# Layer 1 of a two-layer encoder: all four condition vectors weighed by VectorE, slabs and ring turns in another order

## What is computed

```
for layer in range(2):
    mod = silu(c) @ w_ada[layer] + b_ada[layer]          # 1024 -> 6 x 1024
    sh1, sc1, g1, sh2, sc2, g2 = split(mod, 6)
    h = rmsnorm(x, mix_norm_g[layer]) * (1 + sc1) + sh1
    y = even_mixer(h) if layer == 0 else odd_mixer(h)     # attention + convolution | differential attention
    x = x + g1 * y
    h = rmsnorm(x, ffn_norm_g[layer]) * (1 + sc2) + sh2
    x = x + g2 * hierarchical_moe(h)                      # 32 experts, 2 for each token
```

## Time and profile before

| what | us |
|---|---|
| median of three runs | 1234.25 |
| the profiled execution's own time | 1233.65 |
| its span, first to last instruction | 1231.6 |
| TensorE busy | 891.0 (72%) |
| VectorE busy | 340.9 (28%) |
| ScalarE busy | 170.4 (14%) |
| weights' DMA queue, share of 16 engines | 95.2% |

### The profile page before, as it was taken

How to read it: one execution, slowest core, us unless ns; L and a number is a source line. 1 busy time by engine, 2 the same in 40 slices (tenths; PEclk the granted TensorE clock), 3 DMA queues, 4 the chain that set the end, 5 groups by cost and what they waited for, 6 DMA issues and landing times.

```text
span 1231.6 us, 14489 instructions
## 1 busy us (share of the span) xinstructions
PE 891.0 (72%) x5990; PEld 431.9 (35%) x5990; DVE 340.9 (28%) x879; ACT 170.4 (14%) x409; POOL 23.8 (2%) x70
## 2 busy tenths in 40 slices
PE   6999998657474756566799999967465565665647
PEld 5867453122221312121278555533121212121212
DVE  3298445121211111111133653521111111202111
ACT  1123340000000000000033253400000000000000
POOL 1001100000000000000000100000000000000000
PEclk9999999787887868787899999989787878888778
DMA  9999989999999999999996838999999999999997
GB/s 349 397 404 408 412 350 423 427 429 427 427 429 427 428 428 429 427 429 428 405 408 233 321 137 317 378 426 427 428 427 427 428 429 428 428 430 426 428 423 283
DMA packets 62136, 490.05 MB, mean 398 GB/s; under 512 B 5600, under 2 KB 6001, under 8 KB 39552
## 3 DMA queue, kind: packets, MB, share of 16 engines
q1 hardware_dynamic: 59568, 486.56, 95.2%
q10 hardware_dynamic: 2512, 2.69, 0.6%
HBM read 488.18 MB, written 1.05 MB: 397 GB/s over the span
## 4 chain that ended last, share of the span: by engine, by line
DMA 49%; PE 42%; DVE 3%; SPq 2%; ACT 2%; issue 1%; POOL 0%; DVEq 0%; ACTq 0%
PE psum L1598 42%; DMA weight_ring<-in_moe_w_up 16%; DMA weight_ring<-in_moe_w_down 16%; DMA weight_ring<-in_moe_w_gate 16%; SPq L489 2%; DMA weight_ring<-in_w_ada 1%; ACT phase_region L893 1%; DVE h_or_mix_T L1111 0%; PE psum L1697 0%; POOL phase_region L660 0%; DVE ada_partials L1522 0%; DVE phase_region L1554 0%; ACT phase_region L1012 0%; DVE phase_region L1081 0%; DVE h_or_mix_T L1243 0%
## 5 line engine op out<-in xcount | busy, mean ns | idle before, releaser
L1598 PE MATMUL psum<-weight_ring,h_or_mix_T 128*32 128x512 f32 (+1 forms) x2240 | 383.3, 709 | 231.7 <-DMA weight_ring<-in_moe_w_gate 142.0
L1598 PEld LDWEIGHTS psum<-weight_ring,h_or_mix_T 128*32 128x32 f32 (+1 forms) x2240 | 118.7, 136 | 478.5 <-issue 476.6
L1598 PE MATMUL psum<-weight_ring,ada_partials 128*32 128x512 f32 x1024 | 138.9, 699 | 77.9 <-DMA weight_ring<-in_moe_w_down 72.9
L1598 PE MATMUL psum<-phase_region 128*128 128x128 f32 (+5 forms) x816 | 154.3, 351 | 6.1 <-DVE phase_region L1424 1.6
L1598 PEld LDWEIGHTS psum<-phase_region 128*128 128x128 f32 (+2 forms) x816 | 97.9, 188 | 79.5 <-issue 53.8
L1598 PE MATMUL psum<-h_or_mix_T,weight_ring 128*128 128x256 f32 (+1 forms) x528 | 115.0, 374 | 2.8 <-DVE h_or_mix_T L1111 2.7
L1598 PEld LDWEIGHTS psum<-h_or_mix_T,weight_ring 128*128 128x128 f32 x528 | 97.3, 190 | 17.5 <-DVE h_or_mix_T L1111 1.9
L1598 PEld LDWEIGHTS psum<-weight_ring,ada_partials 128*32 128x32 f32 x1024 | 38.8, 126 | 165.4 <-issue 158.2
L1424 DVE TENSOR_TENSOR phase_region<-psum,gate_rows 128x512 f32<-128x512 f32 x32 | 22.1, 692 | 224.7 <-PE psum L1598 224.7
L1411 DVE SCALAR_TENSOR_TENSOR phase_region<-phase_region,psum 128x512 f32<-128x512 f32 x16 | 11.0, 687 | 236.9 <-ACT phase_region L925 236.9
L1416 DVE SCALAR_TENSOR_TENSOR ada_partials<-phase_region,psum 128x512 f32<-128x512 f32 x16 | 16.8, 1050 | 209.3 <-PE psum L1598 209.3
(11 more groups left out here) (220 smaller groups left out, 479.5 us busy)
## 6 DMA issues: line engine op xcount, KB each, us to landing
weight_ring<-in_moe_w_up SPq DMA_DIRECT2D x64, 2048.0 KB, 20.5
weight_ring<-in_moe_w_gate SPq DMA_DIRECT2D x62, 2048.0 KB, 19.9
weight_ring<-in_moe_w_down SPq DMA_DIRECT2D x62, 2048.0 KB, 20.0
weight_ring<-in_w_ada SPq DMA_DIRECT2D x10, 3072.0 KB, 20.3
weight_ring<-in_odd_w_in SPq DMA_DIRECT2D x6, 2048.0 KB, 23.9
weight_ring<-in_w_ada SPq DMA_DIRECT2D x10, 1024.0 KB, 22.4
weight_ring<-in_w_ada SPq DMA_DIRECT2D x4, 2048.0 KB, 17.9
weight_ring<-in_even_w_in SPq DMA_DIRECT2D x3, 2048.0 KB, 21.0
```

The costliest lines, as they stand in the source:

```text
L1598: return pe.matmul(out_, lhsT, rhs, start=first, stop=last, **kw)
```

## The change

Vectors 10 and 11 go the way of 8 and 9: VectorE weighs the slab, TensorE only adds partitions. All four are now weighed between the projections, in the order 8, 9, 10, 11; their slabs, the ring's places and layer 1's turns are reordered; `gate_join` of layer 1 gives way to `keep_warm(1, 16)`. Two pieces of layer 0's mixer change place. The end of each layer loads and multiplies the last down quad in other pieces (two loads of two experts with rows 0 and 1, then left halves of rows 2 and 3, then the right side in columns 512 to 767 and 768 to 1023), and the copy into `CREP1` is gone.

```diff
-        mid_slabs = [("odd_in", 0, 1, proj_done, 26), ("odd_in", 1, 2, proj_done, 34), ("odd_in", 2, 0, proj_done, 38),
-                     ada(8, 3), ada(9, 1), ("odd_out", 0, 3, wout_done, 8), ada(10, 2), ada(11, 0)]
-        TURNS = [(1, 2, 0, 3), (1, 2, 0, 3)]
+        mid_slabs = [("odd_in", 0, 1, proj_done, 26), ada(8, 2), ("odd_in", 1, 0, proj_done, 34),
+                     ("odd_in", 2, 3, proj_done, 38), ada(9, 2), ada(10, 1), ada(11, 2), ("odd_out", 0, 1, wout_done, 8)]
+        TURNS = [(1, 2, 0, 3), (0, 2, 3, 1)]
...
-                for k in range(2):
+                for k in range(2 + L):
...
+            weigh(8, 0, 5)
+            behind_unit = {0: (8, 5, 6), 1: (8, 6, 7), 2: (8, 7, 8), 7: (9, 0, 2), 8: (9, 2, 4), 9: (9, 4, 6), 10: (9, 6, 8),
+                           11: (10, 0, 1), 12: (10, 1, 2), 13: (10, 2, 4), 14: (10, 4, 6), 15: (10, 6, 8)}
             for u in range(16):
...
-                if 8 <= u < 12:
-                    weigh(8, 2 * (u - 8), 2 * (u - 7))
-                if u == 13:
-                    take_modulation(8)
-                if u > 13:
-                    weigh(9, 2 * (u - 14), 2 * (u - 13))
-
-            weigh(9, 4, KD)
+                if u in (6, 12):
+                    take_modulation({6: 8, 12: 9}[u])
+                if u in behind_unit:
+                    weigh(*behind_unit[u])
+
+            weigh(11, 0, 5)
...
             biased(0)
+            weigh(11, 5, KD)
             biased(1)
-            take_modulation(9)
+            take_modulation(10)
...
-                if u == 14:
+                if u == 5:
                     add_rows(8)
+                if u == 12:
+                    pe.wait_ge(ada_ready, 9)
+                    add_rows(9)
...
+            pe.wait_ge(qk_rstd, 16)
+            add_rows(10)
             scores(0)
             project_values(1, AFT)
             scores(1)
-            pe.wait_ge(qk_rstd, 16)
-            add_rows(9)
...
-                if h == 3:
-                    pe.wait_ge(v_out, 4)
-                    modulation_sums(10)
...
-                if L:
-                    modulation_sums(6 * L + 5, 0, KD // 2)
-                modulation_sums(6 * L + 5, KD // 2, KD)
                 if L == 0:
+                    modulation_sums(5, KD // 2, KD)
                     keep_warm(1, 5)
+                else:
+                    pe.wait_ge(router_ready, 2 * L + 2)
+                    add_rows(11)
+                    keep_warm(1, 8)
...
-                gate_join(6 * L + 5)
+                if L == 0:
+                    gate_join(5)
+                else:
+                    keep_warm(1, 16)
...
             modulation_sums(3)
+            modulation_sums(7, 0, 3)
...
             tails(1)
-            modulation_sums(7)
+            modulation_sums(7, 3, KD)
...
+            pe.wait_ge(logs_min, NPAIR)
+            mix_out(0, 2, (0, 1))
             values(3)
-            for u in (2, 3):
-                mix_out(0, u, (0, 1))
+            mix_out(0, 3, (0, 1))
             pe.wait_ge(ada_ready, 5)
             mix_out(0, 1, (0, 1))
             pe.wait_ge(conv_added, 2)
             channel_sum(S).then_inc(conv_var, 1)
```

The new end of a layer on TensorE (`rows` multiplies one row of four experts, `combine_cols` is `combine` for a slice of columns):

```diff
+                    for row in range(2):
+                        for bank, cols in ((6, left), (7, most), (END_BANK, end)):
+                            ins = rows(row, of_pair(row), bank, cols)
+                    ins.then_inc(last_quarters, 1)
+                    pe.wait_ge(last_cols_in, 32 * (L + 1))
+                    rows(2, of_row(2), 6, left)
+                    rows(3, of_row(3), 6, left).then_inc(down_done, 1)
+                    pe.wait_ge(filled(slabs[1], 0), later + landed(slabs[1], 0))
+                    rows(2, of_row(2), 7, most)
+                    rows(2, of_row(2), END_BANK, end).then_inc(last_quarters, 1)
...
+                    combine((UNROLL + 1) % 2, added, y, (0, 1))
...
+                    rows(3, of_row(3), 7, most).then_inc(cols_done, 1)
...
+                    combine_cols(0, 4, most).then_inc(cols_combined, 1)
...
+                    rows(3, of_row(3), END_BANK, end).then_inc(down_done, 1)
...
+                    combine_cols(1, 4, most).then_inc(cols_combined, 1)
...
+                    for t in range(TB):
+                        combine_cols(t, 0, end).then_inc(combined, 1)
```

More of the change, by code:

```diff
@@ L362, in home @@
         def home(n, half):
-            for start in MOE0:
+            for start, turns in zip(MOE0, TURNS):
                 if start <= n < start + 6 * EP:
-                    return (SPOT[n], 0) if half else (SPOT[n - 1] if n > start else TURNS[0][RING - 1], 1)
+                    return (SPOT[n], 0) if half else (SPOT[n - 1] if n > start else turns[RING - 1], 1)
             return SPOT[n], half
@@ L573, in load_experts @@
                     follow(EP // UNROLL - 1, k)
-                for k in range(LAST - RING, LAST + 2 - RING):
-                    sp.wait_ge(*slab_free(k % 6 // 2, EP * (L + 1)))
-                    for half in range(2):
-                        load_quarter(L, k + RING, half)
+                load_last_down(L)
             sp.dma_start(CCOL[:, 0, :], c.rearrange("o (p k) -> p (o k)", k=KD)).then_inc(cond_in, 16)
@@ L595, in _ @@
             overflow_loads(sp, 0)
-            for n in range(len(mid_slabs) - 1):
+            for n in range(len(mid_slabs)):
                 m = occupant(MID0 + n)
@@ L1421, in quad @@
                         spread(i * UNROLL + (EP * L + j + 1 - L), (j + 1) % 2)
+                    if last:
+                        finish_columns(n)
+                        return
                     for h in range(2):
@@ new lines, in narrow_last, with rows, of_pair @@
+                    y, added = 2 * (EP + 1) * (L + 1), ADDS * (L + 1) - 4
+                    def rows(row, w, bank, cols):
+                        for e in range(WIDE):
+                            ins = mm(PS[e * SLOT:(e + 1) * SLOT, bank, 0:cols.stop - cols.start],
+                                     HIDT[:, row, e * SLOT:(e + 1) * SLOT], w(e, cols), row == 0, row == KF - 1,
+                                     skip_group_check=True)
+                        return ins
+                    def of_pair(row):
+                        return lambda e, cols: by_pair(region(slabs[0], e // 2))[:, e % 2, row * D + cols.start:row * D + cols.stop]
@@ new lines, in of_row @@
+                    def of_row(row):
+                        return lambda e, cols: by_quarter(region(slabs[1], row - 2))[:, e, cols]
+                    left, most, end = slice(0, HALF), slice(HALF, MOST), slice(MOST, D)
+                    for half in range(2):
+                        pe.wait_ge(filled(slabs[0], half), later + landed(slabs[0], half))
+                    for row in range(2):
+                        for bank, cols in ((6, left), (7, most), (END_BANK, end)):
+                            ins = rows(row, of_pair(row), bank, cols)
@@ new lines, in narrow_last @@
+                    combine((UNROLL + 1) % 2, added, y, (0, 1))
+                    pe.wait_ge(filled(slabs[1], 1), later + landed(slabs[1], 1))
+                    rows(3, of_row(3), 7, most).then_inc(cols_done, 1)
+                    pe.wait_ge(cols_scaled, L + 1)
+                    pe.wait_ge(x_added, added + 1)
+                    combine_cols(0, 4, most).then_inc(cols_combined, 1)
+                    pe.wait_ge(end_cols_in, 16 * (L + 1))
+                    rows(3, of_row(3), END_BANK, end).then_inc(down_done, 1)
@@ new lines, in narrow_last, with combine_cols @@
+                    pe.wait_ge(x_added, added + 2)
+                    combine_cols(1, 4, most).then_inc(cols_combined, 1)
+                    pe.wait_ge(y_ready, y)
+                    for t in range(TB):
+                        combine_cols(t, 0, end).then_inc(combined, 1)
+                def combine_cols(t, bank, cols):
+                    return mm(PS[:, bank + t, 0:cols.stop - cols.start], SWT[:, (UNROLL + 1) % 2, t, :], YS[:, cols],
+                              True, True, skip_group_check=True)
```

150 lines of the change are left out of this document (76 added, 74 removed).

## The result

The changed kernel takes 1238.86 us (median of 9 runs, 1237.15 to 1242.36) against 1234.25 for the kernel before in the same rounds: ratio 1.0041, 95% interval [1.0031, 1.0050]. It is slower, where no measurable change was forecast, and lies 0.26 us outside the stated range. The profiled execution took 1239.41 us, with a span of 1237.7. Of all executions of all versions in this document one, of one_a_head, was slow (1498.6 us at a mean granted clock of 0.55); the ratios leave it out, and without it that version's median is 1228.16 instead of 1228.28.

What follows compares the result with a forecast made beforehand. A relay bounds the kernel: DMA where it streams, TensorE's chain where the ring is full. Terms -2.75 + (5.6 - 1.3) - 0.4 = +1.15 us on 1233.65 give 1234.8, median 1235.4; range 1231.2 to 1238.6.

Steps and rivals of the forecast that it cites:

- Layer 0's mixer: Layer 0: blocks moved into two TensorE idle gaps bring channel_sum(S) and the gather 2.75 us earlier.
- The pause before unit 12 with its releaser: Layer 1's projections: TensorE waits 4.3 us for VectorE to finish vector 9.
- The pause before the first transposes: Layer 1, before the heads: TensorE idles some 3 us, released by VectorE.
- the end's chain from row 2's landing: Kernel end: from the landing that releases row 2 to the last add, 10.3 us instead of 10.7.
- the 1.3 us: Layer 1's gather: 0.54 MB still queued hides the first 1.3 us of any delay.
- The 1.8 us to a dry queue's "first byte": Layer 1's gather: a queue run dry moves its first byte about 1.8 us after the issue.
- it decides from a rest of 4 us: Clock rival's limit: TensorE's clock fell after some 4 us of rest near the kernel's end; 4.3 is at the edge.
- The routing: Layer 1, behind the logits: +0.2 for replaced sums, +2.0 for 16 identity matmuls holding back the gather.
- up to the heads: Layer 1, projections to first transposes: VectorE's added k-rows start the head loop 7.2 us later, including the 4.3 pause.
- The rival "the clock falls": Pause before unit 12: TensorE at 1.2 GHz afterwards loses 2.0 us more, or the pause is longer; 1237.4, chance 0.28.
- The rival of layer 0 giving nothing: Layer 0's mixer: a late input of the moved blocks or channel_sum cancels the gain; 1238.1, chance 0.09.
- The faster rival: Layer 1: prefetch keeps the delay from the DMA stream, or unit 12's pause does not arise; 1231.1, chance 0.18.

Runs made afterwards that it cites:

- one_a_head: Changed kernel, vector 9 requested before unit 13, 7 not 16 identity matmuls before the gather, vector 11's last three k-rows behind heads 0 to 2: 1228.28 us.
- warm_both: Changed kernel plus 14 identity matmuls in the pause before unit 12 and 13 before the first head's wait: 1234.80 us, ratio to before 1.0000.
- warm12: Changed kernel plus 14 identity matmuls in TensorE's pause before unit 12: 1236.19 us, ratio to before 1.0018.
- layer0_only: Kernel before with only the two moved pieces of layer 0's mixer: 1231.79 us, ratio to before 0.9979.
- unit13: Changed kernel with vector 9 asked for and taken one unit later, at unit 13 instead of 12: 1233.11 us, ratio to before 0.9988.
- eleven_in_heads: Changed kernel with all eight k-rows of vector 11 weighed two behind each of heads 0 to 3: 1240.28 us, ratio to before 1.0044.
- all_three: Changed kernel with the edits of unit13, short_warm and eleven_in_heads together: 1232.77 us, ratio to before 0.9983.
- short_warm: Changed kernel with seven instead of sixteen identity matmuls before layer 1's gather: 1237.48 us, ratio to before 1.0024.

## Why the prediction was wrong

**Right, step by step.** Layer 0's mixer (-2.75, measured -2.75). The pause before unit 12 with its releaser (4.3 forecast, 4.13 of idling measured). A small miss: vector 8's request cost a wait of 0.31 where none was forecast. The pause before the first transposes (some 3, measured 3.48), released by VectorE. The 32 identity instructions before the gather. Behind the gather, 1.7 in all forecast and 1.9 measured; the end's chain from row 2's landing is 10.2 us, forecast 10.3. Only the number of the 1.3 us is right: it was read as a part of any delay that is hidden, and that 4 MB more are loaded early was put at nothing, where one_a_head shows that the early loads themselves are worth 1.5 us without a delay. The 1.8 us to a dry queue's "first byte" are a starting point worked out as if the queue ran at full rate at once; the trace has 33 GB/s already over 680.0 to 680.5, some 1 us after the issue at 679.40, and 328 GB/s only over 681.25 to 681.5. The sum is not touched by this.

**The failed step** is the one on the clock. The sum of the likeliest case has no term for TensorE's clock. Pauses were priced by their length alone, as if the work behind them ran at full speed. The loss was written down as a rival, for one pause only, with a price of 2.0 and the sentence "it decides from a rest of 4 us". Measured are 1.7 behind the pause of 4.13 us (unit 12 takes 5.35 instead of 3.62) and 3.1 behind the one of 3.48 us (head 0 takes 8.62 instead of 5.53), and 4.7 in the stretch when both losses are taken away (warm_both). So the price of one fall was about right. The second pause was forecast, some 3 us, and even listed among the signs, but it was not priced, because it lay below the limit of 4 us. This limit came from one rest near the kernel's end: the mean of 0.64 places the fall at 1198.6, 4.0 us after the last matmul. One rest gives no limit, and the same trace has others that speak against this one:

```profile
466.72 2.70 PE L1598 MATMUL psum<-phase_region 128*128 128x512 f32 x5
471.25:471.50 0.25, 0.00 (x0) 0.00 (x0) 0.00 (x0) 0.00 (x0) 0.00 (x0) 1.00 0.92 393
471.50:471.75 0.25, 0.00 (x0) 0.00 (x0) 0.00 (x0) 0.00 (x0) 0.00 (x0) 0.53 1.24 524
```

The last matmul ends at 469.42, and the clock is low from 471.5, 2.1 us later. In the 40 rests of 5.2 to 11.6 us of this trace the fall comes 2.1 to 5.4 us after the last matmul. So a fall could have been expected in a rest of 3 us too, though not with certainty. In the changed kernel the clock was low from 716.25, 3.2 us into the rest and before TensorE restarted at 716.54.

**The mis-sized term.** The routing was priced at 0.2 + 2.0 = 2.2 us. From the end of the logits to the gather it is 784.27 - 777.90 = 6.37 before and 791.93 - 784.37 = 7.56 after, so 1.2: the 16 identity matmuls advance TensorE by 3.65 us (788.28 to 791.93) and not by 4.1, and a wait of 0.30 for ScalarE's copy went with `gate_join`; these two are 0.75 of the 1.0.

**The balance of the stretch,** forecast against measured: up to the heads +7.8 (7.2, and the 0.6 ahead of the projections) against +8.4 (warm12's 92.91 less 84.53), the wait at vector 8 being 0.3 of the difference; clock behind unit 11, 0 against 1.7; clock in head 0, 0 against 3.1; the loop -3.66 against -3.6; the routing 2.2 against 1.2. The measured ones add up to 10.8, and 10.79 was read. The forecast ones add up to 6.3, and not to the 6.2 behind the forecast, which rounds its gather to +5.6 where its terms make 5.7. On the profiled execution the account closes: 1234.8 forecast, 4.6 more in the stretch, 0.2 less gained ahead of it (-3.13 at the start of the projections, forecast -3.35) and 0.2 more gained behind it make 1239.4, and 1239.41 was measured. The median lies 0.55 below that execution, where the forecast put it 0.6 above; so it was luck that the range was missed by only 0.26 us.

The rival "the clock falls" (1237.4, chance 0.28) is thus the one that came true, but it had one fall of the two. The rival of layer 0 giving nothing is refuted by layer0_only. The faster rival, that the prefetch carries the delay, is refuted by unit13, which gets back in the median all that it saves in the pause and its clock, and by the windows of 0 GB/s before the gather: the ring is full and waits for TensorE. Of the 9.8 us of lead that this rival named, 1.5 us were gained.

The Trainium skill, page "TensorE: Matmul & The Clock Gate", section "HAM oscillation — how this bites in real kernels", says that a transition of the clock is paid again at every gap that is long enough, not once in a kernel. The traces agree: one fall for each of the two pauses, and each filler takes away its own. They also show a fall without a long gap, in eleven_in_heads and all_three, where no rest in the loop is over 1.79 us.

## What to carry to other kernels

Price every pause that a change makes on TensorE twice: its length, and what the work behind it loses at 1.2 GHz (1.7 and 3.1 us here for rests of 4.1 and 3.5 us), and look at many rests of the trace before calling one too short. Several short rests close together can cost a fall too (eleven_in_heads). Where a change moves work onto another engine inside a tight hand-over, count how much of that engine is free between two hand-overs: here one k-row of 1.3 us nearly fitted and two did not, and eleven_in_heads and one_a_head, which also differ by unit13's and short_warm's edits, are 12 us apart. And a new request placed one unit too early costs its wait and a fall of the clock, and is cured by placing it one unit later.

## What the runs showed of the hardware

The 28 and 26 identity matmuls of the fillers held the clock at full speed (warm_both, 715 to 725 us, and unit 12 at 3.72), so multiplying the identity counts as work for the clock.

The clock also fell where TensorE had only short rests. In eleven_in_heads it fell at 731.5 us, 1.5 us after the restart from a rest of 1.79 us, with rests of 0.83 and 0.90 before it; in all_three behind the third rest of 1.79. In one_a_head, with rests of 0.83, 0.47 and 0.47, it did not fall.

The two falls in the changed kernel are unlike: the rest of 3.48 us cost more (3.1) than the one of 4.13 (1.7), since the low clock lasted 6.9 us there and 3.4 here. How long it stays low does not follow from the length of the rest. What it costs is near half of the time in which TensorE works at the low clock: 1.7 of 3.4 us, and 3.1 of the 6.5 us from 716.54 on. In unit13 and warm12 the clock fell 2.2 and 2.1 us into the same rest of 3.48, so less work met it, and head 0 lost 2.6.

The time from layer 0's gather to the projections comes at two levels: in these fourteen profiles 447.3 to 448.0 us in eight and 449.4 to 450.1 in six, with versions that don't differ in it on both levels (unit13 447.41, all_three 449.70). That is 2.2 us between executions of the same code, while the stretch of layer 1's mixer repeats to 0.04. What makes it was not found.
